# Eight depth products of the RG gate tile moved between the second-level joins, and the split of v moved to scan step 2

## The reference

```python
h = rmsnorm(x, pre_w) * (1 + scale) + shift
proj = h @ w_in                      # 1024 -> 6176 columns
q, k, v = silu(short_conv(qkv)), q and k normalised     # 8 heads of 128
o_dn = gated DeltaNet, forward and backward, chunked    # triangular solve in each chunk
o_rg = (h_f + h_b) * silu(gate)      # RG-LRU, forward and backward, 8 blocks of 128
y = concat([o_dn, o_rg]) @ w_out
x + mod_gate * rmsnorm(y, post_w)
```

## Time and profile before

| | us |
|---|---|
| median of 3 runs | 1524.68 |
| lowest, highest | 1523.77, 1526.91 |
| the profiled execution's own time | 1524.72 |
| its span | 1523.1 |

### The profile page before, as it was taken

How to read it: one execution, slowest core, us unless ns; L and a number is a source line. 1 busy time by engine, 2 the same in 40 slices (tenths; PEclk the granted TensorE clock), 3 DMA queues, 4 the chain that set the end, 5 groups by cost and what they waited for, 6 DMA issues and landing times.

```text
span 1523.1 us, 24595 instructions
## 1 busy us (share of the span) xinstructions
PE 1391.1 (91%) x8182; PEld 1248.2 (82%) x8182; DVE 1027.9 (67%) x2135; ACT 753.3 (49%) x1912; POOL 115.3 (8%) x135
## 2 busy tenths in 40 slices
PE   5966899999999989999999999899989997599997
PEld 1266898899799879988997998799889976388886
DVE  3565477779677877887797778778877966722222
ACT  2351357564646465565647464745666484511111
POOL 0000100010001000100000010001000000212211
PEclk9978999999799999999999999999999998699999
DMA  8702111110111211111111111102111150523440
GB/s 306 249 14 68 28 29 32 57 44 30 40 49 44 57 48 28 60 33 42 44 44 36 53 44 49 55 22 67 33 42 45 44 225 20 153 77 110 124 123 29
DMA packets 95235, 102.79 MB, mean 67 GB/s; under 512 B 4230, under 2 KB 81271, under 8 KB 94089
## 3 DMA queue, kind: packets, MB, share of 16 engines
q1 hardware_dynamic: 92170, 90.70, 19.4%
q0 software_dynamic: 2944, 10.49, 1.8%
HBM read 85.88 MB, written 15.29 MB: 66 GB/s over the span
## 4 chain that ended last, share of the span: by engine, by line
PE 77%; ACT 8%; DVE 6%; issue 5%; DMA 3%; SPq 0%; DVEq 0%; ACTq 0%
PE bank L673 14%; PE bank L675 14%; PE bank L674 14%; PE bank L947 12%; PE bank L901 2%; PE bank L868 2%; PE bank L784 2%; PE bank L909 2%; PE bank L917 2%; PE bank L894 2%; PE bank L889 2%; PE bank L824 2%; DMA arena<-pos_row 2%; PE bank L746 1%; ACT L1089 1%
## 5 line engine op out<-in xcount | busy, mean ns | idle before, releaser
L673 PE MATMUL bank<-hT_hi,w_hi 128*128 128x384 f32 (+1 forms) x1224 | 442.0, 361 | 30.9 <-DVE w_lo L1379 17.6
L675 PE MATMUL bank<-hT_hi,w_lo 128*128 128x384 f32 (+1 forms) x1224 | 419.4, 343 | 0.0
L674 PE MATMUL bank<-hT_lo,w_hi 128*128 128x384 f32 (+1 forms) x1224 | 419.4, 343 | 0.0
L673 PEld LDWEIGHTS bank<-hT_hi,w_hi 128*128 128x128 f32 x1224 | 235.8, 193 | 33.7 <-DVE w_lo L1379 18.5
L674 PEld LDWEIGHTS bank<-hT_lo,w_hi 128*128 128x128 f32 x1224 | 235.9, 193 | 1.2
L675 PEld LDWEIGHTS bank<-hT_hi,w_lo 128*128 128x128 f32 x1224 | 234.9, 192 | 0.0
L1225 ACT ACTIVATE arena<-bank,arena 128x128 f32<-128x128 f32 x272 | 78.7, 369 | 176.2 <-PE bank L901 176.0
L1469 DVE SCALAR_TENSOR_TENSOR arena<-arena 128x1154 f32<-128x1154 f32 x96 | 137.5, 1433 | 3.5 <-DVE arena L1467 1.1
L947 PE MATMUL bank<-wo_hi,ot_hi 128*128 128x512 f32 x288 | 114.3, 397 | 18.8 <-DVE ot_lo L1758 13.5
L947 PE MATMUL bank<-wo_lo,ot_hi 128*128 128x512 f32 x288 | 113.6, 395 | 0.0
L947 PE MATMUL bank<-wo_hi,ot_lo 128*128 128x512 f32 x288 | 113.3, 393 | 0.0
(11 more groups left out here) (224 smaller groups left out, 2388.4 us busy)
## 6 DMA issues: line engine op xcount, KB each, us to landing
w_raw<-w_in SPq DMA_DIRECT2D x51, 512.0 KB, 4.0
arena<-ada_w SPq DMA_DIRECT2D x8, 1536.0 KB, 10.8
arena<-scr_G SPq DMA_DIRECT2D x16, 576.0 KB, 4.8
ot<-scr_o SPq DMA_DIRECT2D x9, 1024.0 KB, 6.7
arena<-x_sample SPq DMA_DIRECT2D x16, 512.0 KB, 7.3
wo<-w_out SPq DMA_DIRECT2D x4, 2048.0 KB, 16.0
scr_o<-arena POOLq DMA_DIRECT2D x8, 576.0 KB, 4.2
arena<-pos_row SPq DMA_DIRECT2D x32, 128.0 KB, 5.5
```

Of the source, the lines that this page charges most:

```text
L673: pe.matmul(out, w_hi[:, slot, k], hT_hi[:, k, cols], start=first, stop=False)
L674: pe.matmul(out, w_hi[:, slot, k], hT_lo[:, k, cols], start=False, stop=False)
L675: return pe.matmul(out, w_lo[:, slot, k], hT_hi[:, k, cols], start=False, stop=last)
```

## The change

- `project(128, 16, b)` at the end of phase A becomes `project(128, 8, b)`: n = 17 is left out there.
- n = 17 is done in the next joins stage: behind `join64(0)`, `join64(1)`, `join64(2)` and `join64(3)` PE does two depth products each (six matmuls). It gets bank 7, and waits for the level 0 joins to be taken from it.
- ACT takes n = 17 at the end of its joins program, no longer between the first and the last four block copies into `Zt`.
- `joins_gate(4)` waits for the gate before it as the others do, not for n = 17.
- ACT's split of the v tile moves from scan step 0 to scan step 2, DVE's from scan step 1 to scan step 2. `load_tile(1, b)` is not edited, but what it waits for comes later.

```diff
--- before.py
+++ after.py
@@ -359,7 +359,7 @@
             return w_tile(name, b + ahead)
 
         def proj_bank(n):
-            return banks[(n + (n >= 16)) % 2]
+            return banks[7 if n == 17 else (n + (n >= 16)) % 2]
 
         SCORE_BANKS = (5, 6, 7, 2, 3)
 
@@ -703,8 +703,10 @@
                     if k == 0:
                         if n < 2:
                             pe.wait_ge(gate_tanh.sem, gate_tanh.at(b, 11 + n))
-                        elif n >= 16:
-                            pe.wait_ge(gate_tanh.sem, gate_tanh.next(b, n - 14))
+                        elif n == 16:
+                            pe.wait_ge(gate_tanh.sem, gate_tanh.next(b, 2))
+                        elif n == 17:
+                            pe.wait_ge(dZ_taken.sem, dZ_taken.next(b, 24))
                         else:
                             pe.wait_ge(proj_taken.sem, proj_taken.at(b, n - 1))
                     o, w = GROUPS[g]
@@ -801,7 +803,7 @@
                 pe.wait_ge(conv_done.sem, conv_done.at(b, 3))
                 for i in range(3):
                     gate(i, b)
-                project(128, 16, b)
+                project(128, 8, b)
 
             def joins(b, last=False):
                 pe.wait_ge(turn_taken.sem, turn_taken.at(b, 30))
@@ -857,12 +859,14 @@
                                 joins_gate(i, b)
                         if g > 0:
                             join(g - 1)
+                            if level and g < 5:
+                                project(134 + 2 * g, 2, b - 1)
 
             def joins_gate(i, b):
 
                 d, of_input, (o, n) = i // 6, i % 6 // 3, GROUPS[i % 3]
-                if i in (3, 4):
-                    pe.wait_ge(proj_taken.sem, proj_taken.prev(b, 14 + i))
+                if i == 3:
+                    pe.wait_ge(proj_taken.sem, proj_taken.prev(b, 17))
                 else:
                     pe.wait_ge(gate_tanh.sem, gate_tanh.at(b, i - 1))
                 pe.matmul(banks[i % 2][:, 0:n], wg[:, 2 * of_input + d], xf[:, o:o + n], start=True, stop=True)\
@@ -1157,8 +1161,6 @@
                 for d in range(DIRS):
                     src = block_T if d else block_in
                     act.wait_ge(unblocked.sem, unblocked.next(b, d + 1))
-                    if d:
-                        take_projection(17, b)
                     for q in range(4):
                         r = slice(BLK * q, BLK * q + BLK)
                         act.activation(Zt[r, NCH * d:NCH * d + NCH, r], src[r, NCH * d:NCH * d + NCH, :], ACT.Copy)\
@@ -1211,6 +1213,7 @@
                 gain_root(1, b)
                 take_joined(1, 4)
                 take_joined(1, 5)
+                take_projection(17, b - 1)
 
             def scan(b, last=False):
                 done = [0, 0]
@@ -1224,7 +1227,7 @@
                             c1 = slice(chunk[d], chunk[d] + 1)
                             act.activation(to[:, d], banks[2 + d][:, P:2 * P], ACT.Copy, scale=hcv[scale][:, d, c1])\
                                .then_inc(vnew_made.sem, 1)
-                    if step == 0 and not last:
+                    if step == 2 and not last:
                         high_w(1, w_loaded[1].at(b, 1) * 16)
                     done[1] += SCAN_FILLS[step]
                     while 8 * (done[0] + 1) <= done[1]:
@@ -1650,7 +1653,7 @@
                         rg_piece("scan", 1, b)
                         dve.wait_ge(rg_scanned.sem, rg_scanned.at(b, 6))
                     if not last:
-                        if step == 1:
+                        if step == 2:
                             low_w(1, w_lo_made.at(b, 2))
                         if step == 7:
                             low_w(0, w_lo_made.at(b, 3))
```

## The result

The changed kernel takes 1568.9 us (median of 4 runs, 1567.8 to 1576.5) against 1525.8 for the kernel before; the ratio is 1.0269, interval 1.021 to 1.0327. It is slower by 43 us, not by the 98 that were forecast. The profiled execution is the slowest of the four, 1576.5 us with a span of 1574.9, 51.8 over the span before. So what follows explains 52 us of span, of which the median shows 43.

The account below looks back on a forecast made before the run. PE, with 77% of the chain, was taken to bound the kernel. -1.9 + 10.3 + 4.5 - 1.5 = +11.4 a head gave +91; 1524.7 + 91 + 13 (split) - 9 + 3 = 1623 us, range 1528 to 1690.

Parts of the forecast that it names:

- (b): At the joins' start: the 3.1 us pause drops the clock to half, level 0 +10.3 a head, bounds 0 and 11.5.
- (c): Level 1 of the joins: n = 17 there costs +4.5 us a head, bounds 0 and 12.3; +1.6 without slow clock.
- (a): End of phase A: without n = 17 the joins' first q products start 1.9 us earlier, bounds 0.7 and 1.9.
- rival 2: Clock falls at the joins' start, but only for 3.4 us: +12, 1537 us in all, chance 0.12.
- (d): Behind the joins: with PE denser in level 1 the clock fall goes, -1.5 a head, bounds -1.7 and 0.
- (e): SP's load of the v tile now waits for the last moved group, near level 1's end: costs nothing.
- (f): Scan step 2: DVE's split waits for ACT's, ahead of S's update: +1.9 in 7 heads, bounds 0 and 2.6.
- the low stretches of before, -6 and -3: Taken off the sum: 6 us that low clock in heads 1 and 4 cost already, 3 for head 0's shorter pause.

Follow-up runs that it names:

- the kernel with groups alone: The kernel before, all kept, with 24 throwaway matmuls a head in level 1 at the moved groups' places, heads 0 to 6: 1537.8 us, ratio 1.0086.

## Why the prediction was right or wrong

The direction and the mechanism hold; the size was more than twice too large. The step that failed is the price of the low clock in (b), +10.3 a head for level 0, where the runs showed +6.0 on the average, with its sequel in (c), +4.5 for level 1, where they showed 1.5.

(a) *n = 17 leaves phase A*: PE stood idle 2.96 where 3.1 was said, and phase A is 1.8 shorter where 1.9 was. But "gain 1.9" was wrong. At full clock, in the kernels with the pause filled, level 0 is 17.1 to 17.6 instead of 16.2, since DVE's first take does not come earlier by as much; what is left is some 0.6, just below the lower bound. Before, DVE's first take had 1.56 of idle time ahead of it, and I took PE for its cause, as the row says:

```profile
670.57 0.36 DVE L1619 TENSOR_TENSOR arena<-bank,arena 128x192 f32<-128x192 f32 x1 [1.56 <-PE bank L824]
```

(b) *The fall at q0*: in eight heads of eight, as forecast, and shown by filling the pause and by leaving the groups out. Its price was not. I took +10.3 for level 0, near the bound of 11.5 for a level slow throughout. Measured is +48.5 in eight heads, 6 on the average: +8.3 in four heads, +9.9 in head 6, and +1.7 in heads 3, 4 and 5, which behaved as rival 2 said. I leaned on one case, head 1 before, where the low clock lasted 24 us; there it had come behind the gates of level 0. Where it came at q0 and lasted, it ended behind the pair of gates 6 and 7; the forecast had this as a possibility and gave it 1.2 of the 11.5, where it was worth 3 in four heads. Why it lasted only 3.4 us in three heads stays open; it goes with the instant of the fall, as said above.

(c) *Level 1*: +1.55 at full clock, as worked out (1.6), seen in the kernel with groups alone. I took +4.5, for a low clock that would reach into it. It did so in three heads only, by a second fall, +4.0. In the other five level 1 is 15.4, 0.9 over a usual head; that is less even than 1.55. Without the groups, level 1 behind a slow level 0 is 13.36 (heads 1 to 5), 1.1 under the 14.50 of the kernel before, perhaps because ACT and DVE are ahead then; the groups cost 2.0 on top of that. In all, with the low stretch of head 1 before gone, +11.9 where the sum had 36.

(d) *Behind the joins*: no fall there in heads 0 to 6, step 0 4.63; -8.7 for the -9 of the sum. That they agree so well is partly luck: heads 1 and 4 gave 2.0 each, and head 7 nothing. (e) *SP*: no wait for the tile was seen; ACT's waits for `w_raw` are 50.4 us in all, 50.6 before.

(f) *The split*: +1.9 said, +1.85 measured, in both kernels that have it. What I had not seen is its other side: with the fall in step 0 gone, step 1 would have been 5.9 to 6.5, as the split there runs beside POOL's masks and takes 3.0 to 3.5; taking it out of the step brings 5.6.

*The sum*, head by head of the forecast against all heads measured: level 0 +82 against +48.5; level 1 +36 against +11.9; q0 earlier -15 against -11.5; step 0 -9 against -8.7; the split +13 against +11.7 with step 1; the low stretches of before, -6 and -3, are in the measured differences. The two clock terms are 58 too large, 49 with these 9 taken off; the rest agrees within a few us. What the range got right was to take in rival 2; the chance of 0.70 for a low clock through level 0 in every head was too high, and a mixture of both in one run had no case of its own.

## What to carry to other kernels

Taking work from an engine that runs beside another chain of equal length gains only the difference of their ends, and leaves a pause. On TensorE that pause has a price of its own when small products follow: look at what the granted clock does behind every pause of the trace before you open a longer one, and do not take the length of one low stretch for that of the next. An instruction that moves in time meets other neighbours: DVE's split was 2 us longer beside POOL's masks. When the two halves of a handover stand in one step of a pipelined loop, the second waits for the first with all that is queued behind it; a step between them costs nothing.

## What the runs showed of the hardware

- Useless work made both kernels faster: 17 throwaway matmuls a head in pauses of 1.1 to 1.5 us took 12 us off the kernel before, as the granted clock stayed at 1.00 in all of heads 0 to 6.
- The same pause of 2.9 to 3.1 us ahead of the same instructions was followed by 3.4, 6.8, 20.5 or 23.9 us at half clock, and one of 2.54 by 20.5 or by nothing. An edit that takes 1.85 us of stall out of each head made the kernel no faster: six heads had the longest case. A difference of 1% between two versions of this kernel can be the clock alone; stage lengths at full clock tell what the edit did.
- The clock did not wait for dense projections to come back: in 18 heads it came back behind two gate products side by side (2.7 us, 386 and 384 columns), among small products that had not brought it for up to 21 us. Behind a like pair in level 1 it stayed at 0.50 (head 1 before), with PE busy for 23.29 of 23.80 us.
- DVE's split of one tile took 1.22 us alone, 3.0 with 2.0 us of POOL's affine selects beside it and 3.5 with 2.5: nearly the whole of POOL's time was added.
- At the turn of the loop DVE stood 1.3 to 1.8 us before its first instruction and PE 0.3 to 1.0. That the turn is the cause is read from heads 0 and 7, which stand behind no turn and show no such gap. Beside another wait neither is seen.
